# Layer norms in two token halves inside a chain of FFN and mixer stages on one Trainium2 core

## What is computed

```python
h = layer_norm(h, ln_in_g, ln_in_b)
for l in range(2):
    h = layer_norm(ALPHA * h + 0.5 * swiglu_ffn(h, ffn1_w13[l], ffn1_w2[l]), ln_g[l, 0], ln_b[l, 0])
    h = layer_norm(ALPHA * h + token_mix(h, w_in[l], ..., w_out[l]), ln_g[l, 1], ln_b[l, 1])
    h = layer_norm(ALPHA * h + 0.5 * swiglu_ffn(h, ffn2_w13[l], ffn2_w2[l]), ln_g[l, 2], ln_b[l, 2])
```

## Time and profile before

| | us |
|---|---|
| median of 3 runs | 3288.42 (3281.95 to 3288.99) |
| the profiled execution | 3287.05 |
| its span, first to last instruction | 3285.3 |
| TensorE busy | 3188.7 |
| VectorE, ScalarE, GpSimd busy | 994.0, 823.5, 1028.9 |
| second block (this change) | from about 1176 to the end |

### The profile page before, as it was taken

The page is one execution under the profiler, slowest core; times in us unless marked ns, Lnnn a source line. Parts: engine busy times, 40 slices in busy tenths (PEclk is TensorE's granted clock), DMA queues, the critical chain, the costliest instruction groups (busy, mean ns, idle before and its releaser), DMA issues.

```text
span 3285.3 us, 53116 instructions
## 1 busy us (share of the span) xinstructions
PE 3188.7 (97%) x23542; PEld 2560.1 (78%) x23542; DVE 994.0 (30%) x1652; ACT 823.5 (25%) x1112; POOL 1028.9 (31%) x453
## 2 busy tenths in 40 slices
PE   7999999999999989999999999999999999999998
PEld 4465689644444479999997999999999999778885
DVE  2144766531212141111463311113111164321113
ACT  2042412110000042222422422224222233242223
POOL 1020256200000023333462333333333346244431
PEclk9999999999999999999999999999999999999999
DMA  7541000359999932222211222222222222122221
GB/s 313 200 128 52 27 3 2 131 205 428 429 428 429 428 135 83 98 83 71 95 61 52 78 93 87 93 74 83 99 81 93 78 78 77 52 77 103 77 90 45
DMA packets 37744, 438.48 MB, mean 133 GB/s; under 512 B 5910, under 2 KB 6678, under 8 KB 11542
## 3 DMA queue, kind: packets, MB, share of 16 engines
q1 hardware_dynamic: 36088, 433.94, 33.7%
q10 hardware_dynamic: 1444, 1.36, 0.2%
HBM read 432.41 MB, written 2.10 MB: 132 GB/s over the span
## 4 chain that ended last, share of the span: by engine, by line
PE 60%; DVE 2%; ACT 1%; POOL 1%; DVEq 0%; issue 0%; ACTq 0%
PE PS L2399 42%; PE PS L2396 10%; PE PS L2638 2%; PE PS L2408 2%; PE PS L2210 1%; PE PS L2672 1%; PE PS L2656 1%; PE PS L2216 1%; DVE high L2270 1%; POOL w_lo L2386 1%; DVEq L2308 0%; ACT w_hi L2381 0%; PE PS L2633 0%; DVE low L2298 0%; PE PS L2681 0%
## 5 line engine op out<-in xcount | busy, mean ns | idle before, releaser
L2386 POOL TENSOR_TENSOR w_lo<-low,w_hi 128x2048 fp32r<-128x2048 f32 (+2 forms) x168 | 737.8, 4391 | 1664.9 <-ACT w_hi L2381 1664.5
L2399 PE MATMUL PS<-h_hi,w_hi 128*128 128x264 f32 x2736 | 561.0, 286 | 3.5 <-DVE h_lo L2979 3.4
L2399 PE MATMUL PS<-h_lo,w_hi 128*128 128x264 f32 x2736 | 558.8, 286 | 0.0
L2399 PE MATMUL PS<-h_hi,w_lo 128*128 128x264 f32 x2736 | 558.2, 285 | 0.0
L2399 PEld LDWEIGHTS PS<-h_hi,w_hi 128*128 128x128 f32 x2736 | 425.7, 188 | 8.9 <-issue 8.3
L2381 ACT ACTIVATE w_hi<-low 128x2048 fp32r<-128x2048 f32 (+2 forms) x168 | 306.8, 1826 | 493.6 <-PE PS L2399 397.4
L2399 PEld LDWEIGHTS PS<-h_lo,w_hi 128*128 128x128 f32 x2736 | 424.6, 188 | 0.0
L2399 PEld LDWEIGHTS PS<-h_hi,w_lo 128*128 128x128 f32 x2736 | 424.3, 189 | 0.0
L2508 DVE TENSOR_TENSOR low<-low,PS 128x528 f32<-128x528 f32 (+1 forms) x84 | 58.8, 700 | 778.6 <-PE PS L2399 576.3
L2399 PE MATMUL PS<-g_hi,w_hi 128*128 128x264 f32 (+1 forms) x1056 | 221.9, 291 | 1.6 <-POOL w_lo L2386 1.6
L1851 PE MATMUL PS<-arena 128*64 128x512 f32 x1024 | 223.1, 593 | 0.3 <-DMA arena<-wts_dram 0.3
(11 more groups left out here) (392 smaller groups left out, 4414.8 us busy)
## 6 DMA issues: line engine op xcount, KB each, us to landing
arena<-wts_dram SPq DMA_DIRECT2D x108, 2048.0 KB, 18.2
low<-wts_dram SPq DMA_DIRECT2D x70, 2048.0 KB, 7.7
arena<-wmod_dram SPq DMA_DIRECT2D x9, 2048.0 KB, 8.1
low<-wts_dram SPq DMA_DIRECT2D x12, 1536.0 KB, 6.4
arena<-na_bias_dram SPq DMA_DIRECT2D x16, 512.0 KB, 3.6
arena<-x_dram SPq DMA_DIRECT2D x2, 2048.0 KB, 8.5
low<-wts_dram SPq DMA_DIRECT2D x2, 1024.0 KB, 5.2
out_dram<-high SPq DMA_DIRECT2D x8, 256.0 KB, 2.5
```

Source lines behind the costliest of these rows:

```text
L2386: nc.gpsimd.tensor_tensor(lo, raw, hi.bitcast(F32), ALU.subtract).then_inc(w_l.sem, 1)
L2399: mm = nc.tensor.matmul(bank(b, h), w[wi], halves(x[xi])[:, h, :], start=(first and i == 0), stop=(last and i == 2))
```

## The change

1. `GROUPS` is 6, 8, 8 hidden tiles instead of 8, 8, 6.
2. In the five norms between stages the output tiles 4 to 7 are made half by half (`UNITS`): tiles 0 to 3 whole, then tiles 4 to 7 for tokens 0 to 263 (half A), then tiles 4 to 7 for half B. The statistics of half A are summed and spread at hooks inside half B's products, those of half B at hooks inside the opening of the next stage (`HOOKS`, `ln_half_pe`, `FIRST_ORDER`).
3. The next stage opens with three products, first all of half A, then half B (`first_three`, in the `fin` stage as well, there with matmuls of 248 and 264 columns). `h_lo` is made by POOL alone, from a copy `hT` that ACT writes for all tiles.
4. The opening's four weight tiles and the last four output tiles come in pieces of 1024 columns; the buffer for pieces is four quarters of 1024 columns, and a piece waits for whatever was last in its quarters.
5. The input norm has no half products before it but is scaled half by half; the last norm keeps its order.

```diff
-GROUPS = [(0, 8), (8, 8), (16, FT - 16)]
+GROUPS = [(0, 6), (6, 8), (14, FT - 14)]
...
+BOTH, ONE, SINGLE = (2 * D, 2), (D, 2), (D, 1)
...
+                    add_chunk([SINGLE] * 4 if f0 + c == 0 else [BOTH] * 2)
+            for c in range(DNC):
+                n = DK // DNC * nf * P // 2
+                add_chunk([SINGLE] * 4 if f0 + nf == FT and c == DNC - 1 else [(n, 2)] * 2)
...
+    UNITS = [(m, None) for m in range(4)] + [(m, h) for h in range(2) for m in range(4, DK)]
+    SQUARED = [(4, 0), (5, 0), (0, None), (1, None), (2, None), (6, 0), (3, None), (7, 0)] + [(m, 1) for m in range(4, DK)]
+    FIRST_ORDER = ([("hi", 0, k, (0,)) for k in range(5)] + [("sums", 1), ("hi", 0, 5, (0,))] + [("hi", 0, k, (1,)) for k in range(6)] + [("mean", 1)] +
+                   [("hi", 0, k, (0, 1)) for k in (6, 7)] + [("inverse", 1)] + [("hi", 0, k, (2,)) for k in range(DK)] +
+                   [("lo", 0, k, (0, 1, 2)) for k in range(DK)] + [("hi", 1, k, (0, 1)) for k in range(DK)] +
+                   [("hi", 1, k, (2,)) for k in range(DK)] + [("lo", 1, k, (0, 1)) for k in range(DK)] + [("lo", 1, k, (2,)) for k in range(DK)])
...
+    HOOKS = {(4, 0, 3): [("first", 3)], (4, 0, 6): [("spread",)],
+             (7, 0, 5): of_half("square", range(4), None) + of_half("square", (4, 5, 6), 0) + of_half("rest", (4, 5, 6), 0),
+             (4, 1, 4): [("rest", 7, 0), ("square", 7, 0)], (5, 1, 1): [("mean", 0)], (5, 1, 6): [("inverse", 0)],
+             (7, 1, 4): of_half("rest", (4, 5, 6), 1) + of_half("square", (4, 5, 6), 1)}
+    HOOKS_MIX = {**HOOKS, (3, None, 2): [("first", 0), ("first", 1)], (3, None, 5): [("first", 2)]}
...
+            split(0)
+            square(4, 1)
+            split(1)
+            high_part(0, 0)
+            high_part(0, 1)
+            full_copy(0, 0)
+            square(5, 1)
+            high_part(0, 2)
+            full_copy(0, 1)
+            split(2)
+            high_part(0, 3)
+            full_copy(0, 2)
+            square(6, 1)
...
+            moments(1)
+            full_copy(0, 6)
+            root(1)
+            full_copy(0, 7)
+            split(3)
...
-        if i >= 2:
-            product_done, n = last_product[i - 2]
+        occupant = next((x for x in range(i - 1, -1, -1) if quarters(x) & quarters(i)), None)
+        if occupant is not None and (l is not None or i > 3):
+            product_done, n = last_product[occupant]
...
+                if f == 0:
+                    scale_res(act, l, 2 * w - 1)
+                    split_act(act, l, i + 4)
+                elif f > 1:
                     split_act(act, l, i + 1)
```

More of the change, by code:

```diff
@@ L2045, with add_chunk @@
 CSIZE, PIECES = [], []
[L2048 to L2057, removed]
+quarter = 0
+def add_chunk(pieces):
+    global quarter
+    at = 0
+    for n, room in pieces:
+        PIECES.append((len(CSIZE), at, n, quarter % 4))
+        quarter += room
+        at += n
+    CSIZE.append(at)
+BOTH, ONE, SINGLE = (2 * D, 2), (D, 2), (D, 1)
 for kind in ("ffn", "mixer", "ffn"):
@@ L2198, in centred, with quads @@
         else:
[L2199 to L2209, removed]
+            summed(eng, l, uu, k, h)
+    def quads(b, at, x, first, last, mean="mean_d", js=range(4)):
+        for j in js:
             mm = nc.tensor.matmul(PS[32 * j:32 * j + 32, b, at:at + QN], C[mean][:, 0:32], x[:, j * QN:(j + 1) * QN], start=first, stop=last)
@@ L2327, in ln_act @@
[L2327 to L2332, removed]
-            ln_n.wait(act, l, uu, k + 1)
-            if l == NL - 1 and uu == 2:
+        nc.scalar.activation(cq, PS[:, R_BANK, 0:QN], ACT.Copy, scale=2.0).then_inc(ln_cs.sem, 1)
@@ L2335, in ln_act @@
+        for k, h in SQUARED[0:8] if halved(l, uu) else [(k, None) for k in SQUARES]:
+            square(k, h)
+        moments(0)
+        root(0)
+        if last_norm(l, uu):
+            for k in range(DK):
+                ln_n.wait(act, l, uu, k + 1)
                 nc.scalar.activation(hT[:, k, :], res[:, k, :], ACT.Identity, bias=shift[:, k:k + 1]).then_inc(ln_f.sem, 1)
@@ L2342, in ln_act, with ln_pool, low @@
         nc.scalar.activation(ashift, shift, ACT.Copy, scale=ALPHA)
-    def ln_pool(pool, l, uu):
-        if l == NL - 1 and uu == 2:
+    def ln_pool(pool, l, uu, split):
+        if last_norm(l, uu):
             return
-        for k in range(DK - LOV):
-            ln_h.wait(pool, l, uu, k + 1)
-            ln_f.wait(pool, l, uu, k + 1)
-            nc.gpsimd.tensor_tensor(h_lo[:, k, :], hT[:, k, :], h_hi[:, k, :].bitcast(F32), ALU.subtract).then_inc(ln_lp.sem, 1)
+        def low(h, k):
+            ln_f.wait(pool, l, uu, h * DK + k + 1)
+            nc.gpsimd.tensor_tensor(part(h_lo[:, k, :], h), part(hT[:, k, :], h), part(h_hi[:, k, :], h).bitcast(F32),
+                                    ALU.subtract).then_inc(ln_lp.sem, 1)
+        if l is not None:
+            split(0)
+            split(1)
+        for k in range(DK):
+            if l is not None and k == 3:
+                split(2)
+            low(0, k)
+        if l is not None:
+            split(3)
+        for k in range(DK):
+            low(1, k)
@@ L2390, in weights, with product @@
         return piece(i)[2:]
-    def product(b, w, x, first, last, fin=False):
+    def product(b, w, x, first, last, fin=False, hs=range(2)):
         for i, (wi, xi) in enumerate([(0, 0), (0, 1), (1, 0)]):
@@ L2605, in mix_pe @@
                 i, j = where[kind, t]
[L2606 removed]
+                if j == 0 and kind != "xp":
                     wt = weights(pe, l, S_MIX + i)
             if kind == "xp":
[L2609 removed]
+                for last in first_three(pe, l, 0, S_MIX):
                     last.then_inc(u_ps.sem, 1)
@@ L2822, in mix_act @@
         mixed_hi(7)
-        split_act(act, l, S_OUT + 2)
-        split_act(act, l, S_OUT + 3)
+        for i in range(2, 6):
+            split_act(act, l, S_OUT + i)
     def mix_pool(pool, l):
@@ L2830, in mix_pool @@
         nc.gpsimd.drain().then_inc(xz_sb.sem, 1)
-        for i in range(2, 5):
+        for i in range(4, 7):
             split_pool(pool, l, S_MIX + i)
@@ L2865, in mix_pool @@
             mixed_lo(k)
-        for i in range(S_OUT + 2, S_FFN2 + 2):
+        for i in range(S_OUT + 2, S_FFN2):
             split_pool(pool, l, i)
```

475 lines of the change are left out of this document (318 added, 157 removed).

## The result

The changed kernel takes 3296.08 us (median of 9 runs, 3292.92 to 3297.49) against 3287.36 of the kernel before (9 runs, 3281.95 to 3288.99): ratio 1.0024, 95% interval 1.0015 to 1.0032. It is slower by 0.24%, where 6.8 us less had been forecast, and it lies outside the stated range of 3274 to 3289. The profiled execution took 3297.3, 10.25 more than the one of before.

What follows compares the result with a forecast made beforehand. PE's stream was taken as the bound, with 27 us to win at five norms. 13.9 won in norms, less 6.2 for groups and 0.9 for the input norm, gave 6.8 us won: 3281.6 us median, range 3274 to 3289.

Steps and rivals of the forecast that it cites:

- Matmuls and sums stay as many: In the norms between stages: the change leaves the number of PE's matmuls and sums as it was.
- PE work of the norm: 7.6 us against 7.45: In each norm between stages: PE's work beside the products grows only from 7.45 to 7.6 us.
- The groups, 6.2 us lost: Last group's first down piece, four FFN stages: 2048 columns split late, 1.56 us exposed a stage, 6.2 lost.
- hidden in the wait for DVE: Norm windows before the change: PE's fall to the lower clock costs no time of its own, so no term.
- The waits in a norm: PE's waits in norms: 0.9 at the centre's spread behind FFNs, others at a square and behind the opening.
- square (6, B): Half B's square of tile 6 on ACT comes late: PE waits 0.65 us behind a mixer, 0.25 behind an FFN.
- the piece behind the opening: First 2048-column weight piece after each opening: 0.55 us wait, bounds 0 and 1.2; 0.3 more in the `fin` stage.
- the rival of pieces and queues: Half-width ACT operations cost 0.55 rather than 0.42 us, 4.5 in all: 3286.1, no measured change; 20%.
- that of ACT as the bound: In every norm, half-width ACT operations at 0.65 to 0.73 us make PE late: 17 us, 3299; 9%.
- The switch of tables drains: Table load behind two queued pieces, three FFNs: ACT's pipeline must empty first, 3.8 us more, 3285.4; 4%.
- The input norm, 0.9 lost: Input norm, scaled by halves: loss 0.4 us, 0.9 with a stretch at the lower clock; bounds -1 and 2.5.
- 13.9: Five norms between stages: 2.0 us won behind each of three FFNs, 4.35 and 3.55 behind the mixers, together 13.9.

Runs made afterwards that it cites:

- e7: e2 with the value sums of each half on the two groups of 32 output rows its squares leave free; 3273.35 us, ratio to before 0.9959.
- e2: The change with the last group's first four output tiles' down weights in four pieces of 1024 instead of two of 2048; 3280.68 us, ratio to before 0.9983.
- e10: The change with only the value sums of each half moved to the output rows its squares leave free, down pieces of 2048 kept; 3288.02 us, ratio 0.9997.
- e1: The kernel before with only the groups of hidden tiles changed to 6, 8 and 8; 3295.68 us, ratio to before 1.0029.
- e3: The change with the norm's sums laid out in matmuls of 66 columns instead of 132, four for a half; 3295.40 us, ratio 1.0025.
- e5: The kernel before with groups 6, 8 and 8 and the last group's first down weights in four pieces of 1024; 3283.38 us, ratio 0.9988.
- e6: The kernel before, groups kept, with the last group's first down weights in four pieces of 768 instead of two of 1536; 3285.71 us, ratio 0.9994.
- e8: The change with the squares of output tiles 0 to 3 also summed by halves, all first halves, then all second; 3298.24 us, ratio 1.0029.
- e9: e7 with the two kinds of half sums issued one kind after the other instead of in turn; 3276.34 us, ratio 0.9958.

## Why the prediction was wrong

By its own steps:

- *The sum's first line, "Matmuls and sums stay as many", and "PE work of the norm: 7.6 us against 7.45".* This failed, and it is the larger miss. As many matmuls, but a sum's four run beside one another, so half of them save nothing: 8 sums became 16 of 0.23 to 0.25, about 2.0 us a norm, 10 in all. e7 gets 7.3 of them back on e2 and e10 8.1 on the change. The earlier trace rows had shown the price of a whole, 0.24 for four, which one matmul of 132 columns costs too; I had halved it without asking whether the four were serial. The rest of the 2.65 (2.05 by which the windows are over, 0.6 of forecast waits that did not come) is put down to more hooks to enter and leave, each some 0.3 of time beside its own matmuls, and to half spreads of 0.47 to 0.65 where I had put 0.45; no run takes these apart.
- *The groups, 6.2 us lost.* The wait was sized right: (2.03 - 0.53) x 3 and 2.33 - 0.83, 6.0 us. The term left out the clock, which I had dismissed as "hidden in the wait for DVE": true of the norm in the earlier trace rows, not of a wait with products queued behind it. Three falls of 1.5 are 4.5 us; for the last stage, from its first down product to the end of the span, it is 78.7 in the change against 77.2 in e1 and e3, which waited there as long and did not fall. e1 measures +8.5 for the groups, e2 and e5 that both go with a smaller first piece. It also cost the change its centre: 0.54 of wait behind each FFN.
- *The waits in a norm.* Right in direction, too large in size: 0.54 at the centre for 0.9, none at square (6, B) for 0.25 and 0.65, 0.27 to 0.62 at the piece behind the opening for 0.55, and 0.85 in the `fin` stage as forecast. A half-width operation on ACT took 0.42 (squares) to 0.51 (`h_hi`), on DVE 0.42 to 0.49. The 0.51 is over the 0.5 that the prediction had named as a sign of being wrong, but no wait of PE in these norms came of it:

```profile
L2447 ACT ACTIVATE h_hi<-high 128x264 fp32r<-128x264 f32 x96 | 48.4, 509 | 13.5 <-DVE high L2339 13.5
...
L2339 DVE SCALAR_TENSOR_TENSOR high<-high,PS 128x264 f32<-128x264 f32 x96 | 46.3, 489 | 19.5 <-PE PS L2236 14.8
...
L2431 ACT ACTIVATE low<-high 128x264 f32<-128x264 f32 x40 | 16.7, 419 | 55.4 <-DVE high L2730 35.3 <-DVE high L3210 20.1
```

  So neither the rival of pieces and queues (0.55) nor that of ACT as the bound (0.68) was what happened, although the time landed beyond the former's; the slower outcome came by a way not among the rivals.
- *The switch of tables drains.* It did not. The load behind two queued pieces takes 1.28, and the next operation of ACT starts at its end:

```profile
2212.60 1.28 ACT L2452 ACT_TABLE_LOAD   x1
2213.89 0.20 ACT L2452 ACTIVATE low<-high 128x1 f32<-128x1 f32 x1
2214.00 0.26 ACT L2454 ACTIVATE low<-PS 128x132 f32<-128x132 f32 x1
```

- *The input norm, 0.9 lost.* 1.8 by the two profiles, 2.2 between e5 and e2. The opening starts 1.3 earlier, counted from the norm's first sum, and ACT's pace is the 0.91 assumed (`h_hi` at 1195.58, 1196.49, 1197.39). What was sized too small is the clock: PE, fed one tile at a time, runs the opening at the lower level for 6.6 us where before it was some 3.5. Behind the paced stretch 15 matmuls still take 0.22 instead of 0.12, 1.5 us for the 0.5 that the sum had. Granted clock of the change, 2 us each:

```profile
1196.00:1198.00 2.00, 1.66 (x5) 1.04 (x5) 1.85 (x5) 2.00 (x6) 2.00 (x3) 0.50 0.01 4
1198.00:1200.00 2.00, 1.90 (x7) 1.60 (x8) 1.93 (x6) 2.00 (x5) 2.00 (x4) 0.50 1.01 238
1200.00:1202.00 2.00, 2.00 (x11) 2.00 (x11) 1.85 (x5) 2.00 (x6) 2.00 (x3) 0.50 0.98 418
1202.00:1204.00 2.00, 2.00 (x16) 2.00 (x16) 1.78 (x6) 2.00 (x6) 1.90 (x4) 0.82 0.92 393
```

- *Not in the sum at all:* the first block, whose instructions the change leaves alone, ended 3.0 us later in this profile. Over the profiles of the twelve kernels it ended between 1171.0 and 1178.3, so that is scatter, not the change; the medians, 8.7 apart, hold less of it.

The account of the profiled executions: forecast -6.8; windows 2.05 longer in four norms and 1.7 in the fifth, +9.9; falls of the clock +4.5; first block +3.0; input norm +0.9; first down piece -0.2 (6.0 for 6.2); piece behind the opening -0.4 (2.6 in five stages for 3.05): +10.9, against +10.25 measured. The 0.65 between them isn't placed.

What the halves were to win by themselves, 13.9 - 0.9 = 13.0 us, came to 2.7 as built (e2 against e5) and to 10.0 with the two kinds of sums side by side (e7 against e5): the main idea held, and the step that failed is the price of half a sum.

## What to carry to other kernels

Before half an operation is priced at half its time, look at whether its parts run one after another: matmuls onto separate groups of 32 output rows run beside one another, so the busiest group sets the cost, and two kinds of half sums belong on different groups. A wait of 2 us on an engine that otherwise streams costs more than 2 us once its clock falls behind it, so a first weight piece that nothing covers, as that of the last group here, should be small. The change hid the norm's waits as it was meant to and lost more than that elsewhere; with both repaired it gives 0.41%. Where the wait was only 0.5 to 0.8 us, smaller pieces gave nothing that could be measured (e6).

## What was not expected of the hardware

- Five kernels here have the same waits for the first down piece, 2.03 us in three stages and 2.33 in the fourth. Behind them PE's granted clock fell three times of four in the change and in e8 (stages 1, 3, 4), and two of four in e1 (1, 3), e3 (1, 2) and e10 (2, 4), 12 of 20 in all, and never behind the waits of 0.53 to 0.83 at the same place before. So it isn't the stage that decides. Why the same wait is spared once and not another time is open.
- Small matmuls on different output rows overlap even when one is issued eight behind the other (e8), and six behind (e9) with some loss, 0.5 us a norm. How far this reaches was not tried.
- With 128 x 128 weights a spread's matmul of 66 columns costs 0.20, as one of 132 columns does (0.81 for four of either). From which width on the columns count was not tried.
